# Moving a small fold matmul and a set of transposes to earlier places in a long product loop

## The reference

```python
# first block: half FFN, mLSTM mixer, half FFN
h = h + 0.5 * rmsnorm(swiglu(rmsnorm(h, g0), ffn_w_in[0], ffn_w_out[0]), g1)
h = h + rmsnorm(mlstm_mixer(rmsnorm(h, g2), ...), g3)
h = h + 0.5 * rmsnorm(swiglu(rmsnorm(h, g4), ffn_w_in[1], ffn_w_out[1]), g5)
# second block: two layers
for l in range(2):
    mod = silu(c) @ w_ada[l] + b_ada[l]            # one row of 3072
    shift, scale, gate = jnp.split(mod, 3, axis=-1)
    h = rms_norm(x, pre_norm_g[l]) * (1.0 + scale) + shift
    proj = h @ w_in[l]
    ...                                            # attention, gated convolution
    x = x + gate * rms_norm(mix @ w_out[l], post_norm_g[l])
```

## Time and profile before

| | |
|---|---|
| median of 3 runs | 801.04 us (800.56 to 802.61) |
| the profiled execution | 801.04 us, span 799.2 us |
| PE busy | 789.4 us, 99% of the span |
| DVE busy | 579.2 us, 72% |
| ACT busy | 419.6 us, 53% |
| POOL busy | 122.3 us, 15% |
| mean granted clock of TensorE | 0.996 |

### The profile page before, as it was taken

One profiled execution on the slowest core, in us unless ns is written; L12 is line 12 of the kernel. 1 busy time (PEld: TensorE's weight loads), 2 busy tenths in 40 slices (PEclk: granted clock), 3 DMA queues, 4 the chain that ended last, 5 costly groups with the idle time before them and its releaser, 6 DMA issues.

```text
span 799.2 us, 14899 instructions
## 1 busy us (share of the span) xinstructions
PE 789.4 (99%) x5944; PEld 748.8 (94%) x5944; DVE 579.2 (72%) x924; ACT 419.6 (53%) x731; POOL 122.3 (15%) x139
## 2 busy tenths in 40 slices
PE   9999999999999999999999999999999999999997
PEld 8999999999999999999999988889999987999985
DVE  6877776699687976778777777976576666567753
ACT  7544444454358565655444443457655557556541
POOL 3800000032320000020000000010054411035510
PEclk9999999999999999999999999999999999999999
DMA  9866666695426642548866769635454570744531
GB/s 326 310 256 242 219 241 245 213 326 181 142 78 224 203 146 81 185 154 283 309 231 227 270 202 390 197 137 179 142 182 132 161 260 23 244 158 128 158 110 53
DMA packets 45188, 158.80 MB, mean 199 GB/s; under 512 B 5040, under 2 KB 6576, under 8 KB 45120
## 3 DMA queue, kind: packets, MB, share of 16 engines
q1 hardware_dynamic: 45120, 157.85, 58.7%
HBM read 156.76 MB, written 1.06 MB: 197 GB/s over the span
## 4 chain that ended last, share of the span: by engine, by line
PE 94%; DVE 3%; issue 1%; ACT 1%; DMA 1%; POOL 0%; SPq 0%; DVEq 0%; POOLq 0%; ACTq 0%
PE ps L344 24%; PE ps L346 23%; PE ps L345 23%; PE ps L777 4%; PE ps L778 4%; PE ps L776 4%; PE ps L717 1%; PE ps L614 1%; PE ps L688 1%; PE ps L707 1%; PE ps L397 1%; PE ps L697 1%; PE ps L389 1%; PE ps L385 1%; PE ps L386 1%
## 5 line engine op out<-in xcount | busy, mean ns | idle before, releaser
L1146 DVE TENSOR_TENSOR w<-raw,w 128x1024 fp32r<-128x1024 f32 x237 | 287.8, 1225 | 135.7 <-ACT w L820 135.3
L344 PE MATMUL ps<-u,w 128*128 128x256 f32 (+1 forms) x1287 | 368.7, 286 | 0.0
L346 PE MATMUL ps<-u,w 128*128 128x256 f32 (+1 forms) x1287 | 365.3, 284 | 0.0
L345 PE MATMUL ps<-u,w 128*128 128x256 f32 (+1 forms) x1287 | 364.8, 283 | 0.0
L820 ACT CAST w<-raw 128x1024 fp32r<-128x1024 f32 x237 | 246.1, 1052 | 112.7 <-PE ps L346 80.5
L344 PEld LDWEIGHTS ps<-u,w 128*128 128x128 f32 x1287 | 242.6, 189 | 6.3 <-issue 4.3
L346 PEld LDWEIGHTS ps<-u,w 128*128 128x128 f32 x1287 | 242.9, 189 | 0.0
L345 PEld LDWEIGHTS ps<-u,w 128*128 128x128 f32 x1287 | 242.2, 188 | 0.1
L1807 POOL TENSOR_SCALAR Sb<-Sb,st 128x256 f32<-128x256 f32 x32 | 45.2, 1427 | 96.3 <-DVE st L1575 96.3
L1164 DVE SCALAR_TENSOR_TENSOR acc<-adr,cact,acc 128x1024 f32<-128x1024 f32 x42 | 55.7, 1341 | 4.2 <-DMA adr<-wada 4.2
L863 ACT ACTIVATE si<-tmp 128x272 f32<-128x272 f32 (+1 forms) x44 | 18.7, 425 | 70.4 <-DVE tmp L1253 70.4
(11 more groups left out here) (262 smaller groups left out, 1040.6 us busy)
## 6 DMA issues: line engine op xcount, KB each, us to landing
raw<-wst SPq DMA_DIRECT2D x245, 512.0 KB, 4.6
adr<-wada SPq DMA_DIRECT2D x48, 512.0 KB, 4.1
Bt<-bias_rows SPq DMA_DIRECT2D x8, 192.0 KB, 3.8
hT<-xT SPq DMA_DIRECT2D x4, 272.0 KB, 5.4
outT<-hT SPq DMA_DIRECT2D x4, 256.0 KB, 2.0
cs<-cst SPq DMA_DIRECT2D x1, 140.0 KB, 5.5
cs<-cst SPq DMA_DIRECT2D x1, 128.0 KB, 6.8
vc<-vec SPq DMA_DIRECT2D x1, 101.0 KB, 3.7
```

Of the source, the lines that this page charges most:

```text
L344: e.matmul(out, a, x1, start=first, stop=False)
L345: e.matmul(out, a, x2, start=False, stop=False)
L346: return e.matmul(out, b, x1, start=False, stop=last)
L1146: e.tensor_tensor(b, raw[:, k % NRAW, :], a.bitcast(F32), ALU.subtract).then_inc(*tick(s_split, k))
```

## The change

PE's `ada_sums(1)` moves from behind P17 to behind P13, and writes to bank 4 in place of bank 6. H1 moves from behind P20 to behind P19. DVE's `modulation(1)` and `layer_gains(1)` move from step 18 to step 14. Layer 0's fold already used bank 4, and nothing of it changes. No instruction is added or removed, and the folds stay in DVE's steps 10 to 12.

```diff
             def ada_sums(l):
                 e.wait_ge(s_fold.handle, 16)
                 e.wait_ge(s_part.handle, at(s_part, (l, 2)))
-                b = place(("ada", l), (4, 6)[l])
+                b = place(("ada", l), 4)
...
-                    if s == "f1" and i == early:
+                    if s == "f1" and i == early - 4:
                         ada_sums(1)
-                    if s == "f1" and i in (early - 1, early + 3):
+                    if s == "f1" and i in (early - 1, early + 2):
                         rows_of_h(int(i > early))
...
-                    m = e.tensor_tensor(mod[p, 24 * l:24 * l + 24], ps[p, (4, 6)[l], 256 + a:352:4],
+                    m = e.tensor_tensor(mod[p, 24 * l:24 * l + 24], ps[p, 4, 256 + a:352:4],
...
-                    if i == NF - 4:
+                    if i == 14:
                         modulation(1)
                         layer_gains(1)
```

## The result

The changed kernel takes 806.48 us (median of 4 runs, 805.91 to 807.17) against 801.18 us of the kernel before (4 runs, 800.56 to 802.61): 5.3 us more, ratio 1.0064 (95% interval 1.0046 to 1.0082, that is 3.7 to 6.6 us). The forecast was 804.2 us with a range up to 806.0. The direction was right; the size was too small, and the time lies above the range.

A forecast was written before the change was run, and what follows sets the result against it. The prediction took PE's own instruction list to bound the kernel. From 801.04 us it added 3.15 for the fold matmul's stall and 0 for each of the other two parts, giving 804.2 us, range 802.9 to 806.0.

The forecast's parts named there:

- What bounds the kernel: Whole span: PE, busy 99%, sets the time; its waits add up to only 3.7 us in 799.
- That the new order makes PE wait, where, and for what: Ahead of the fold matmul (L415), PE waits close to 2.8 us for DVE's third fold.
- That nothing gives the stall back: Behind 511 us, no later PE wait hangs on an absolute time such as a DMA, so all stays.
- fold matmul behind P13: At the moved fold matmul: P14 starts 3.36 us late, less 0.19 saved, taken as 3.15; bounds 1.9 to 3.5.
- The clock: Behind the stall: half clock for 3.4 us would lose 1.5 us; held less likely, no cost in the 804.2 us.
- the likeliest case: Plain stall at the moved fold matmul without clock loss: 804.2 us, own range 803.6 to 804.8, chance 0.65.
- The boundary at 213 to 216: Earlier boundary, taken as clock evidence: 21 small matmuls and 0.6 us wait, then clock 0.50 over 216.2 to 219.6.
- Bank 4, modulation in step 14: H0's wait for modulation's bank 4 read stays hidden with nearly 6 us; later splits still in time: zero cost.
- H1 behind P19: The same transposes before P20 instead of behind it: zero, or a small gain if chunk 21's DMA is late.
- (a): Rival: the clock drops in most executions behind the stall, 805.7 us; chance 0.22.
- (b): Rival: the stall at the fold matmul is small or absorbed, 802.9 us or 801.4 us; chance 0.10.
- (c): Rival: faster, an earlier fold frees H1 from waiting for modulation through bank 6; gain 0.6, 800.4 us; chance 0.03.

The follow-up runs named there:

- the second trace: The changed kernel profiled once more, with no edit: 805.35 us, span 803.5 us (one run).
- the fold matmul alone: The kernel before with one edit, the fold matmul moved behind P13, bank 6, modulation and H1 as before: 807.03 us, ratio 1.0067.
- the filler: The changed kernel with 30 unused matmuls put behind P13, ahead of the wait for the third fold: 804.85 us, ratio 1.0039.

## Why the prediction was wrong

*What bounds the kernel* held: PE's list of instructions is the time, and a stall of PE is paid in full.

*That the new order makes PE wait, where, and for what* held: ahead of L415, for the third fold, with P13 ending at 508. That nothing gives the stall back held too (5.66 us at the last product of tile 1, 5.7 us at the end).

*The term "fold matmul behind P13"*: 3.15 us predicted, with 3.5 as its upper bound; measured 3.21 in one trace and 4.29 in the other. From the end of the fold to P14 it took 0.54 and 0.72 us, where the prediction's terms make 0.58 in the same count, so that part was right to 0.15 us. That the second trace agrees to 0.06 us is partly luck: a fold that came 0.1 us sooner against P13, and a slower start of P14. What was mis-sized is when the fold ends, 3.94 us behind P13 in the first trace in place of 2.78. I took it from one execution, asked only what would make it earlier (no DMA wait), and let the upper bound come from the refill. In the kernel before the fold had 7.9 us to spare, so its scatter (1.65 us over the nine traces) did not reach the measured time; the change used the spare up and made the scatter part of the time. The bound had to be open on both sides.

*The clock* is the step that failed first: the sum of the likeliest case has nothing for it. I priced the drop well for the changed kernel (1.5 us predicted; 1.55 and 1.4 measured, but 2.6 with the fold matmul alone) and held it for a rival at 0.22, arguing that the stall has dense work on both sides. What the runs showed is a drop in every trace (three) with the folds in steps 10 to 12, the fold matmul behind P13 and nothing in the gap. In this stretch it came in all three traces in which PE stood empty for 2.79 us or more (2.79, 2.79, 4.04), and in none with an empty wait of 1.61 us or less (1.61, 1.17, 0.25, and 0.95 behind the filler). The Trainium skill (TensorE: Matmul & The Clock Gate, "Why this matters for your kernels") lists idle gaps between bursts as what brings the half clock back; the trace of the changed kernel agrees, 0.51 of the clock over 512.5 to 515.9. Dense work around the gap didn't save the clock. The boundary at 213 to 216 was a poor model in both directions. PE stood empty there for only 0.59 us, after some 4 us of small matmuls (from 211.1 on), so it was no case of a gap between dense bursts, and the prediction's "the trace agrees at 216.2" says too much. And the drop cost little there, since the chain of waits ran on DVE from 216.41 to 225.99; here every slow product was paid.

*The sum*, from the time of the kernel before in its own trace: 801.04 + 4.29 + 1.55 = 806.9 (806.65 measured in the first trace), and 800.87 + 3.21 + 1.41 = 805.5 (805.35 in the second). The clock alone would have kept the time within the range (804.2 + 1.5 = 805.7); the late fold on top of it, 1.1 us in the first trace, took it out.

*A slip*: the prediction has P16 end at 519.4, while its own start of H0 makes that 519.8. Nothing rests on the 0.4 us.

*Bank 4, modulation in step 14*: zero within the noise, as forecast. Modulation came at 514.12 right behind two splits, H0 at 522.33; PE never waited on a split. *H1 behind P19*: zero within the change, as forecast; alone it costs 1.3 us by the medians, and the chain through bank 6 shows the wait.

*Rivals*: (a) was the case, in both traces of the changed kernel, in the first with a longer stall than it assumed. (b), a smaller stall, occurred in no trace of the changed kernel. (c), a gain by freeing H1 of its wait for bank 6, needed a wait that neither trace of before has.

## What to carry to other kernels

Before an instruction of the bounding engine is moved ahead, compare the end of what it waits for with the end of what stands before it, in several executions: a producer with slack scatters unseen, and the move turns the late side of the scatter into time. Price a stall of TensorE as the wait and a stretch at the lower clock behind it; here 4.0 us of emptiness cost 5.8 us, and 2.8 us cost 4.6 in one trace and 5.9 in another. If a wait can't be avoided, filling it with matmuls that nobody reads can be tried; here 30 of them gave back some 2.3 of 5.3 us, where one or two chunks later on PE gave back nearly all.

## What was not expected of the hardware

The slow stretch behind the stall had different lengths: 8 products (3.4 us) in the changed kernel, 13 (5.6 us) in the kernel with the fold matmul alone, though that one waited less (2.79 against 4.04 us). In the latter the granted clock fell while PE was still empty:

```profile
509.30:511.30 2.00, 0.00 (x0) 0.00 (x0) 1.97 (x3) 1.04 (x1) 0.00 (x0) 1.00 0.37 57
511.50:518.10 6.60, 6.06 (x15) 4.89 (x16) 3.84 (x4) 1.12 (x2) 0.00 (x0) 0.50 0.71 253
```

PE had gone empty at 509.26 and came back at 512.04. So 2.1 us of emptiness were enough for the clock to fall in this execution, less than the whole wait, and between this and the 1.61 us that left the clock alone no run lies.

In steps of 0.1 us the three traces put the fall and the return at 512.4 and 515.8 (changed kernel, PE back at 512.03), 510.8 and 514.2 (the same again, PE back at 510.69) and 511.4 and 518.2 (fold matmul alone, PE back at 512.04). The lower level thus lasted 3.4, 3.4 and 6.8 us, and it lasted twice as long in the one trace in which PE was still empty for 0.65 us after the fall. Three traces don't show that this is the reason. The price of a drop here was 1.4 to 1.6 us or 2.6 us, and it didn't follow the length of the wait.

Why the last `w_ada` DMA lands so differently between executions (the ada_step behind it starts at 498.57 to 500.33) was not tried.
